# Attention: where the sixteen products of the first values unit stand, and where late weight halves are rounded

## The chip, the cores and the metric

The kernel runs on one core of a Trainium2 chip. The metric is the device time of one execution in microseconds. The kernel before took 3226.36 us in the median of three runs (3222.05 to 3228.58).

## The reference, cut to what matters

Two transformer blocks over 256 tokens of width 2048, in float32. The stage of the change is the sparse attention of the first block:

```python
p = rms_norm(x, g_mix) @ w_in
q = rope(rms_norm(q.reshape(B, S, 8, 128), q_gain), pos)      # 8 heads
k = rope(rms_norm(k.reshape(B, S, 8, 128), k_gain), pos)      # 8 heads
v = v.reshape(B, S, 8, 128)                                   # a plain product, no norm
q_idx = rope(q_idx.reshape(B, S, 16, 64), pos)                # 16 index heads of 64
k_idx = rope(k_idx[:, :, None, :], pos)[:, :, 0]
iscore = einsum('bqhd,bsd->bqhs', q_idx, k_idx)
iscore = einsum('bqhs,bqh->bqs', relu(iscore), w_idx)         # summed over index heads
sel = top_k(iscore, 64)                                       # per query, within its chunk's past
out = softmax(q k[sel] * scale) v[sel]
```

## The kernel before, in words

A product of float32 operands is made on TensorE as three fp32r matmuls: high weight half by high input, high weight half by low input, low weight half by high input. `product(u, k)` issues these three for one 128-row slice k of weight unit u (lines 861 to 863). A unit has 16 slices and gives 128 output features for all 256 tokens in one of four banks `PG`. Below, "a product" is one such triple; "half" is half a unit of weights (128 x 1024). Before a half can be used, ScalarE copies it, rounded (`half_high`, line 647), and VectorE subtracts that copy in place (`half_low`, line 652). Four buffers hold rounded copies, so `half_high(h)` waits until the products of half h-4 are done (`half_done` or `unit_done`, line 646).

The input projection has 60 units. Six of them, units 54 to 59 (`V_UNIT` is 54, `LATE` is 6), are the last values heads; their 96 products are left over for the attention, where `values(lo, hi)` (line 1029) issues products lo to hi-1 of them between other work. Halves 108 to 111 (units 54 and 55) are rounded before the attention; halves 112 to 119 (units 56 to 59) in it.

`attention` on TensorE (line 1034) has these stages, all in program order:

- **Squares**: 16 sums over the head dimension, `ones` by the squares of one q or k head (line 1042, a plain float32 matmul that the trace shows as two records). ScalarE squares head n into one of four buffers (line 1655) and waits for sum n-4; VectorE turns sum n into a mean square (line 2243); TensorE's sum n waits for mean n-2. There are no products here.
- **Rope**: 25 rotations (line 1049), the first 9 for the index queries and keys, the other 16 for q and k. Each is followed by two products. VectorE multiplies the rotated tile by the sine (line 2260) and adds the cosine part of GpSimd (line 2263); TensorE's rotation r waits for tile r-2. For tiles 9 to 24, VectorE first applies the norm (line 2250), which needs ScalarE's Ln and Exp over all mean squares (lines 1658 and 1661, two loads of the activation table). VectorE's queue also has `half_low` of halves 112 to 116 ahead of tiles 5, 9, 13, 17 and 21, and of half 117 behind the last (lines 2253 to 2265). ScalarE's queue has `half_high(112)` behind the four Exp.
- **Index**: after four small transposes (line 1055), 32 index products (line 1066), 64 rows deep: 16 heads with 128 keys for the first 128 queries, then 16 with 256 keys for the rest. Each is followed by one product, and the last 14 of the 96 follow alone (line 1069). ScalarE takes relu (line 1682, four buffers), VectorE adds it weighted (line 2277). After each 16, VectorE finds the 64 largest by eight rounds of max and match-replace (lines 2285, 2286).
- **Heads**: transposes of the values (line 1077), then logits, softmax and values of 16 (head, query tile) pairs, with the first products of the output projection between them (from line 1085). The first softmax step is line 2296 on VectorE, after its top-64 search.

All of it is written out by hand; each engine works through its own queue in order. SyncE loads units in turn into four slots, each when its slot's last unit is done (line 740); ScalarE's queue also issues the load of `x` (line 1689) once all values are taken.

Of the kernel before, what the change touches and what calls it, by code (L numbers as in the profile page):

```python
# [15 lines left out]
KT = D // P  # L16
# [241 lines left out]
LATE = 6  # L258
# [8 lines left out]
V_UNIT = P1_AT[("dsa", DSA_TILES - LATE)]  # L267
# [47 lines left out]
def build(nc, A, out):  # L315
    ctx = ExitStack()
    with ctx:
# [41 lines left out]
        def con(name):  # L359
            return C[:, CON[name][0]:CON[name][1]]  # L360
# [277 lines left out]
        HALVES = 2 * U0["wo"]  # L638
# [127 lines left out]
        def _(pe):  # L766
# [262 lines left out]
            def values(lo, hi):  # L1029

                for m in range(lo, hi):
                    product(V_UNIT + m // KT, m % KT)

            def attention():
# [3 lines left out]
                for n in range(16):  # L1038
                    pe.wait_ge(a_sq, n + 1)
                    if n >= 2:  # L1040
                        pe.wait_ge(a_ms, n - 1)
                    pe.matmul(PX[:, n % 2, 0:T], con("ones"), SQ[:, n % 4, :], start=True, stop=True).then_inc(a_sum, 1)

                for r in range(25):
                    if r >= 9:
                        pe.wait_ge(a_nrm, r - 8)
                    if r >= 2:
                        pe.wait_ge(a_rope, r - 1)
                    pe.matmul(PX[:, 2 + r % 2, 0:T], con("perm64" if r < 9 else "perm128"), DQ[:, r, :],
                              start=True, stop=True).then_inc(a_rot, 1)  # L1050
                    values(2 * r, 2 * r + 2)

                pe.wait_ge(a_rope, 25)
                for tt in range(TT):
                    mm = pe.transpose(PX[:, 2, tt * P:tt * P + P], LO[:, 2, tt * P:tt * P + P], con("ident"))
                    mm = pe.transpose(PX[:, 2, T + 32 * tt:T + 32 * tt + 32], RS[0:32, tt * P:tt * P + P],
                                      con("ident")[0:32, 0:32])
                mm.then_inc(a_vt, 1)
                pe.wait_ge(a_v, 1)

                for n in range(TT * IDX_HEADS):
                    tt, h = n // IDX_HEADS, n % IDX_HEADS
                    rows = slice(64 * (h % 2), 64 * (h % 2) + 64)
                    if n >= 4:
                        pe.wait_ge(a_relu, n - 3)
                    pe.matmul(PX[:, h % 4, 0:(tt + 1) * P], DQ[rows, 1 + h // 2, tt * P:tt * P + P],
                              DQ[rows, 0, 0:(tt + 1) * P], start=True, stop=True).then_inc(a_is, 1)
                    values(50 + n, 51 + n)
                values(82, LATE * KT)

                pe.wait_ge(a_relu, TT * IDX_HEADS)
                wait_taken(pe, V_UNIT + LATE - 1)
# [402 lines left out]
        def _(act):  # L1475
# [169 lines left out]
            def attention():  # L1645
# [6 lines left out]
                for n in range(16):  # L1652
                    if n >= 4:
                        act.wait_ge(a_sum, n - 3)
                    act.activation(SQ[:, n % 4, :], DQ[:, 9 + n, :], ACT.Square).then_inc(a_sq, 1)
                for g in range(4):
                    act.wait_ge(a_ms, 4 * g + 4)
                    ins = act.activation(MSB[:, 4 * g:4 * g + 4, :], MSB[:, 4 * g:4 * g + 4, :], ACT.Ln)
# [7 lines left out]
                    act.activation(DQ[:, DSA_TILES - LATE + q, :], PG[:, u % BANKS, 0:T],  # L1666
                                   ACT.Copy).then_inc(free_bank(u), 1)

                for q in range(3):
                    half_high(act, 2 * (V_UNIT + 2 + q))  # L1670
                    half_high(act, 2 * (V_UNIT + 2 + q) + 1)
                    take_v(q)
# [4 lines left out]
                for n in range(TT * IDX_HEADS):  # L1677
                    keys = (n // IDX_HEADS + 1) * P
                    act.wait_ge(a_is, n + 1)
                    if n >= 4:  # L1680
                        act.wait_ge(a_acc, n - 3)
                    act.activation(RL[:, n % 4, 0:keys], PX[:, n % 4, 0:keys], ACT.Relu).then_inc(a_relu, 1)
                    if n in (8, 16):
                        half_high(act, HALVES - 2 + (n - 8) // 8)
                    if n in (16, 31):
                        take_v(3 + n // 31)
                for q in range(5, LATE):
                    take_v(q)
                act.dma_start(XTOK, A["x"]).then_inc(s_xtok, 16)
                for g in range(4):  # L1690
                    act.wait_ge(a_vt, g + 2)
# [285 lines left out]
        def _(dve):  # L1977
# [259 lines left out]
            def attention():  # L2237
# [12 lines left out]
                    dve.scalar_tensor_tensor(DQ[:, r, :], DQ[:, r, :], vec("q_gain" if n < 8 else "k_gain"),  # L2250
                                             MSB[:, n, :], ALU.mult, ALU.mult).then_inc(a_nrm, 1)

                late = dict(zip((5, 9, 13, 17, 21), range(2 * V_UNIT + 4, HALVES)))
                for r in range(25):
                    if r in late:
                        half_low(dve, late[r])
                    if 9 <= r + 1 < 25:
# [4 lines left out]
                    dve.wait_ge(a_cos, r + 1)  # L2262
                    dve.tensor_tensor(DQ[:, r, :], ROPE_S[:, r % 2, :], ROPE_C[:, r % 4, :], ALU.add) \
                       .then_inc(a_rope, 1)
                half_low(dve, HALVES - 3)
                dve.wait_ge(a_v, 1)
                for tt in range(TT):
                    keys = (tt + 1) * P
                    sc = ISC[:, tt, 0:keys]
                    for h in range(IDX_HEADS):  # L2270
                        n = tt * IDX_HEADS + h
                        dve.wait_ge(a_relu, n + 1)
                        w = WX[:, tt, h:h + 1]
                        if h == 0:
                            dve.tensor_scalar(sc, RL[:, n % 4, 0:keys], w, None, ALU.mult).then_inc(a_acc, 1)
                        else:
                            dve.scalar_tensor_tensor(sc, RL[:, n % 4, 0:keys], w, sc, ALU.mult, ALU.add) \
                               .then_inc(a_acc, 1)
                        dve.wait_ge(a_acc, n + 1)
                        if n in (9, 17):  # L2280
                            half_low(dve, HALVES - 2 + (n - 9) // 8)

                    link(dve.memset(ISC[0:CH, tt, keys - CH:keys], NEG))
                    for n in range(TOP_K // 8):
# [654 lines left out]
```

## Time and profile before

| | |
|---|---|
| median of three runs | 3226.36 us |
| the profiled execution | 3221.9 us, of which the span is 3220.0 us |
| TensorE busy | 3091.0 us (96% of the span), 19592 matmuls |
| VectorE busy | 1972.2 us (61%) |
| ScalarE busy | 1503.4 us (47%) |
| GpSimd busy | 211.7 us (7%) |
| mean granted TensorE clock | 0.972 of 2.4 GHz |
| the attention in the span | 585.3 us (first square) to 752.1 us (next stage's first matmul) |

A busy TensorE is not a fast one: its clock has two levels, 2.4 GHz (shown as 1.00) and 1.2 GHz (0.50), and a matmul at the lower level takes twice as long and is busy all the while. Rows of a timeline give the start, the duration and in brackets the idle time before it with what ended it.

### The profile page before, as it was taken

The page shows a single profiled execution, that of the slowest core. Times are in us where ns is not written, and L with a number is a line of the kernel's source. Part 1 is how long each engine was busy: PE and PEld are TensorE (multiplying, and loading weights), DVE is VectorE, ACT ScalarE, POOL GpSimd, SP SyncE. Part 2 cuts the span into 40 slices and gives each one's busy share as a digit, 9 for nine tenths or more (in the row PEclk, how much of TensorE's full clock was granted, in tenths as well). Part 3 has the DMA queues.
Part 4 walks back from the last instruction along what each step waited for, and adds up shares of the span by engine and source line. Part 5 has one row for each costly group of instructions (what it writes and reads, how often), then busy time and mean ns, then how long its engine had stood idle before and what let it go on. Part 6 is the DMA issues. An engine that isn't in the chain of part 4 may idle for free.

```text
span 3220.0 us, 48239 instructions
## 1 busy us (share of the span) xinstructions
PE 3091.0 (96%) x19592; PEld 2731.4 (85%) x19592; DVE 1972.2 (61%) x2533; ACT 1503.4 (47%) x2079; POOL 211.7 (7%) x263
## 2 busy tenths in 40 slices
PE   8999999899799999999997899999999999999998
PEld 7888898667678887777996789999998989899896
DVE  6555655645577787887558874444665545555454
ACT  5445444424466666665530024764444434344343
POOL 0000000200000000000186600000000000000000
PEclk9999999959999999999998998999999999999999
DMA  5222222213288887887442343445555555555554
GB/s 226 86 99 92 102 95 92 79 66 128 102 319 317 313 324 303 319 308 274 170 175 100 118 147 118 162 169 183 210 193 191 190 185 187 192 184 189 186 189 144
DMA packets 81792, 581.80 MB, mean 181 GB/s; under 512 B 9009, under 2 KB 9265, under 8 KB 12338
## 3 DMA queue, kind: packets, MB, share of 16 engines
q1 hardware_dynamic: 79056, 566.45, 48.6%
q10 hardware_dynamic: 2530, 12.36, 1.0%
q8 instruction: 159, 2.61, 0.3%
q14 instruction: 47, 0.39, 0.1%
HBM read 574.58 MB, written 4.19 MB: 180 GB/s over the span
## 4 chain that ended last, share of the span: by engine, by line
PE 82%; DVE 10%; ACT 3%; POOL 2%; issue 2%; DMA 0%; ACTq 0%; SPq 0%; DVEq 0%; POOLq 0%
PE PG L805 9%; PE PG L803 9%; PE PG L806 8%; PE PG L831 5%; PE PG L830 5%; PE PG L829 5%; PE PG L861 4%; PE PG L1234 4%; PE PG L1235 4%; PE PG L1236 4%; PE PG L863 3%; PE PG L862 3%; PE PX L945 3%; DVE work L2599 2%; DVE ring_r L693 1%
## 5 line engine op out<-in xcount | busy, mean ns | idle before, releaser
L693 DVE TENSOR_TENSOR ring_r<-ring,work_r 128x1024 fp32r<-128x1024 f32 x468 | 553.4, 1225 | 320.3 <-ACT work_r L686 317.0
L686 ACT ACTIVATE work_r<-ring 128x1024 fp32r<-128x1024 f32 x468 | 469.0, 1052 | 481.1 <-PE PG L806 236.1
L693 DVE TENSOR_TENSOR ring_r<-ring,C_r 128x1024 fp32r<-128x1024 f32 x244 | 289.3, 1227 | 222.1 <-ACT C_r L686 218.8
L686 ACT ACTIVATE C_r<-ring 128x1024 fp32r<-128x1024 f32 x244 | 245.0, 1052 | 375.5 <-PE PG L806 255.0
L806 PE MATMUL PG<-work_r,ring_r 128*128 128x256 f32 x1344 | 375.1, 279 | 0.0
L806 PE MATMUL PG<-YT_r,ring_r 128*128 128x256 f32 x1280 | 361.8, 283 | 0.0
L863 PE MATMUL PG<-HT_r,ring_r 128*128 128x256 f32 x960 | 276.5, 288 | 0.0
L806 PEld LDWEIGHTS PG<-work_r,ring_r 128*128 128x128 f32 x1344 | 253.5, 189 | 0.0
L830 PE MATMUL PG<-ring_r,HT_r 128*128 128x512 f32 x624 | 246.7, 395 | 0.0
L806 PEld LDWEIGHTS PG<-YT_r,ring_r 128*128 128x128 f32 x1280 | 244.9, 191 | 0.0
L805 PE MATMUL PG<-work_r,C_r 128*128 128x256 f32 x816 | 227.4, 279 | 0.0
L805 PE MATMUL PG<-work_r 128*128 128x256 f32 x800 | 225.2, 282 | 0.0
L803 PE MATMUL PG<-work_r,C_r 128*128 128x256 f32 x672 | 187.5, 279 | 3.2 <-issue 3.2
L803 PE MATMUL PG<-work_r 128*128 128x256 f32 x672 | 188.9, 281 | 0.0
L863 PEld LDWEIGHTS PG<-HT_r,ring_r 128*128 128x128 f32 x960 | 188.1, 196 | 0.0
L803 PE MATMUL PG<-YT_r,work_r 128*128 128x256 f32 x640 | 181.8, 284 | 4.2 <-DVE HT_r L2631 3.5
L803 PE MATMUL PG<-YT_r,C_r 128*128 128x256 f32 x640 | 183.1, 286 | 0.0
L774 PE MATMUL PG<-HT,ring 128*128 128x256 f32 x768 | 172.7, 388 | 0.0
L774 PEld LDWEIGHTS PG<-HT,ring 128*128 128x128 f32 x768 | 149.0, 195 | 24.4 <-issue 3.9
L861 PE MATMUL PG<-HT_r,YT_r 128*128 128x256 f32 x480 | 155.1, 323 | 11.7 <-DVE XT_r L2004 11.7
L805 PEld LDWEIGHTS PG<-work_r,C_r 128*128 128x128 f32 x816 | 153.3, 188 | 0.1
L805 PEld LDWEIGHTS PG<-work_r 128*128 128x128 f32 x800 | 150.5, 188 | 0.0
(619 smaller groups left out, 7599.4 us busy)
## 6 DMA issues: line engine op xcount, KB each, us to landing
ring<-weights SPq DMA_DIRECT2D x472, 1024.0 KB, 4.8
C<-weights SPq DMA_DIRECT2D x32, 1024.0 KB, 4.9
work<-weights SPq DMA_DIRECT2D x32, 1024.0 KB, 5.1
work<-xT SPq DMA_DIRECT2D x4, 512.0 KB, 7.5
XT<-x ACTq DMA_DIRECT2D x1, 2048.0 KB, 9.7
residual<-XT ACTq DMA_DIRECT2D x4, 512.0 KB, 3.0
XT<-residual ACTq DMA_DIRECT2D x1, 2048.0 KB, 10.8
result<-YT SPq DMA_DIRECT2D x8, 256.0 KB, 4.1
```

The source lines that it names most:

```text
L686: act.activation(w_high(u)[:, c], weights(u)[:, c], ACT.Copy).then_inc(w_hi, 1)
L693: dve.tensor_tensor(w_low(u)[:, c], weights(u)[:, c], w_high(u)[:, c].bitcast(F32), ALU.subtract).then_inc(w_lo, 1)
L774: last = pe.matmul(PG[:, (use + t // 2) % BANKS, (t % 2) * T:(t % 2) * T + T], ring[:, u % RING, (k * tiles + t) * P:(k * tiles + t) * P + P],
L803: pe.matmul(o, wh, high[:, k, :], start=(n == 0 and not (down and t_ % 2)), stop=False, skip_group_check=True)
L805: pe.matmul(o, wh, low[:, k, :], start=False, stop=False, skip_group_check=True)
L806: last = pe.matmul(o, wl, high[:, k, :], start=False, stop=(n == kts - 1), skip_group_check=True)
L829: pe.matmul(o, xh, wh, start=(first and kk == 0), stop=False, skip_group_check=True)
L830: pe.matmul(o, xh, wl, start=False, stop=False, skip_group_check=True)
L831: mm = pe.matmul(o, xl, wh, start=False, stop=(last and kk == 3), skip_group_check=True)
L861: pe.matmul(o, wh, HT_r[:, k, :], start=(k == 0), stop=False, skip_group_check=True)
L863: mm = pe.matmul(o, wl, HT_r[:, k, :], start=False, stop=(k == KT - 1), skip_group_check=True)
L1234: pe.matmul(o, xh, wh, start=(k == 0), stop=False, skip_group_check=True)
```

## The change

The 16 products of unit 54 are put between the squares' sums, one behind each. All later products move up by 16: the rope steps issue products 16 to 65, two more (66, 67) follow the last rotation, four (68 to 71) stand behind the small transposes, and the index products take 72 to 95, one each behind the first 24; the last eight index products have none, and nothing is left for behind them. The halves' rounding moves with it: 112 and 113 on ScalarE behind the squares and ahead of Ln; all others up to 119 in the rope stage; on VectorE ahead of tiles 2, 4, 11, 13, 18, 20, one (118) behind the last tile and one (119) behind index product 5. The values of units 54 to 59 are taken out of their banks at matching places.

```diff
--- before.py
+++ after.py
@@ -1040,6 +1040,7 @@
                     if n >= 2:
                         pe.wait_ge(a_ms, n - 1)
                     pe.matmul(PX[:, n % 2, 0:T], con("ones"), SQ[:, n % 4, :], start=True, stop=True).then_inc(a_sum, 1)
+                    values(n, n + 1)
 
                 for r in range(25):
                     if r >= 9:
@@ -1048,14 +1049,16 @@
                         pe.wait_ge(a_rope, r - 1)
                     pe.matmul(PX[:, 2 + r % 2, 0:T], con("perm64" if r < 9 else "perm128"), DQ[:, r, :],
                               start=True, stop=True).then_inc(a_rot, 1)
-                    values(2 * r, 2 * r + 2)
-
+                    values(16 + 2 * r, 18 + 2 * r)
+
+                values(66, 68)
                 pe.wait_ge(a_rope, 25)
                 for tt in range(TT):
                     mm = pe.transpose(PX[:, 2, tt * P:tt * P + P], LO[:, 2, tt * P:tt * P + P], con("ident"))
                     mm = pe.transpose(PX[:, 2, T + 32 * tt:T + 32 * tt + 32], RS[0:32, tt * P:tt * P + P],
                                       con("ident")[0:32, 0:32])
                 mm.then_inc(a_vt, 1)
+                values(68, 72)
                 pe.wait_ge(a_v, 1)
 
                 for n in range(TT * IDX_HEADS):
@@ -1065,8 +1068,8 @@
                         pe.wait_ge(a_relu, n - 3)
                     pe.matmul(PX[:, h % 4, 0:(tt + 1) * P], DQ[rows, 1 + h // 2, tt * P:tt * P + P],
                               DQ[rows, 0, 0:(tt + 1) * P], start=True, stop=True).then_inc(a_is, 1)
-                    values(50 + n, 51 + n)
-                values(82, LATE * KT)
+                    if 72 + n < LATE * KT:
+                        values(72 + n, 73 + n)
 
                 pe.wait_ge(a_relu, TT * IDX_HEADS)
                 wait_taken(pe, V_UNIT + LATE - 1)
@@ -1653,6 +1656,8 @@
                     if n >= 4:
                         act.wait_ge(a_sum, n - 3)
                     act.activation(SQ[:, n % 4, :], DQ[:, 9 + n, :], ACT.Square).then_inc(a_sq, 1)
+                half_high(act, 2 * V_UNIT + 4)
+                half_high(act, 2 * V_UNIT + 5)
                 for g in range(4):
                     act.wait_ge(a_ms, 4 * g + 4)
                     ins = act.activation(MSB[:, 4 * g:4 * g + 4, :], MSB[:, 4 * g:4 * g + 4, :], ACT.Ln)
@@ -1666,7 +1671,8 @@
                     act.activation(DQ[:, DSA_TILES - LATE + q, :], PG[:, u % BANKS, 0:T],
                                    ACT.Copy).then_inc(free_bank(u), 1)
 
-                for q in range(3):
+                take_v(0)
+                for q in range(1, 4):
                     half_high(act, 2 * (V_UNIT + 2 + q))
                     half_high(act, 2 * (V_UNIT + 2 + q) + 1)
                     take_v(q)
@@ -1680,12 +1686,8 @@
                     if n >= 4:
                         act.wait_ge(a_acc, n - 3)
                     act.activation(RL[:, n % 4, 0:keys], PX[:, n % 4, 0:keys], ACT.Relu).then_inc(a_relu, 1)
-                    if n in (8, 16):
-                        half_high(act, HALVES - 2 + (n - 8) // 8)
-                    if n in (16, 31):
-                        take_v(3 + n // 31)
-                for q in range(5, LATE):
-                    take_v(q)
+                    if n in (12, 31):
+                        take_v(4 + n // 31)
                 act.dma_start(XTOK, A["x"]).then_inc(s_xtok, 16)
                 for g in range(4):
                     act.wait_ge(a_vt, g + 2)
@@ -2250,7 +2252,7 @@
                     dve.scalar_tensor_tensor(DQ[:, r, :], DQ[:, r, :], vec("q_gain" if n < 8 else "k_gain"),
                                              MSB[:, n, :], ALU.mult, ALU.mult).then_inc(a_nrm, 1)
 
-                late = dict(zip((5, 9, 13, 17, 21), range(2 * V_UNIT + 4, HALVES)))
+                late = dict(zip((2, 4, 11, 13, 18, 20), range(2 * V_UNIT + 4, HALVES)))
                 for r in range(25):
                     if r in late:
                         half_low(dve, late[r])
@@ -2262,7 +2264,7 @@
                     dve.wait_ge(a_cos, r + 1)
                     dve.tensor_tensor(DQ[:, r, :], ROPE_S[:, r % 2, :], ROPE_C[:, r % 4, :], ALU.add) \
                        .then_inc(a_rope, 1)
-                half_low(dve, HALVES - 3)
+                half_low(dve, HALVES - 2)
                 dve.wait_ge(a_v, 1)
                 for tt in range(TT):
                     keys = (tt + 1) * P
@@ -2277,8 +2279,8 @@
                             dve.scalar_tensor_tensor(sc, RL[:, n % 4, 0:keys], w, sc, ALU.mult, ALU.add) \
                                .then_inc(a_acc, 1)
                         dve.wait_ge(a_acc, n + 1)
-                        if n in (9, 17):
-                            half_low(dve, HALVES - 2 + (n - 9) // 8)
+                        if n == 5:
+                            half_low(dve, HALVES - 1)
 
                     link(dve.memset(ISC[0:CH, tt, keys - CH:keys], NEG))
                     for n in range(TOP_K // 8):
```

## Rows read from the trace of the kernel before

**Rows 1.** The chain of work that ended last: shares of the span by engine.
```profile
PE 82%; DVE 10%; ACT 3%; POOL 2%; issue 2%; DMA 0%; ACTq 0%; SPq 0%; DVEq 0%; POOLq 0%
```
**Rows 2.** Stretches: PE, PEld, DVE, ACT, POOL busy (count), clock, DMA share, GB/s.
```profile
585.86:592.10 6.24, 6.24 (x14) 3.66 (x15) 3.61 (x7) 3.27 (x9) 3.69 (x4) 0.50 0.08 34
...
609.28:612.60 3.32, 3.32 (x11) 2.96 (x12) 1.95 (x5) 0.72 (x1) 0.70 (x1) 0.50 0.00 0
...
643.40:668.42 25.02, 25.02 (x77) 18.19 (x75) 6.80 (x18) 5.11 (x16) 0.00 (x0) 0.50 0.08 28
668.42:701.68 33.26, 33.26 (x82) 19.50 (x81) 13.94 (x43) 7.62 (x19) 0.00 (x0) 0.50 0.11 42
...
712.80:752.10 39.30, 31.21 (x149) 25.24 (x148) 28.06 (x106) 23.31 (x59) 0.00 (x0) 0.83 0.24 85
```
**Rows 3.** Timeline of TensorE: squares' sums, then rotations.
```profile
585.86 6.93 PE L1042 MATMUL PX<-SQ,C 128*128 128x256 f32 x16 [3.84 <-ACT SQ L1655]
...
597.74 0.59 PE L1049 MATMUL PX<-work,C 128*128 128x256 f32 x2
...
598.88 0.60 PE L1049 MATMUL PX<-work,C 128*128 128x256 f32 x2
...
609.28 1.22 PE L1049 MATMUL PX<-work,C 128*128 128x256 f32 x2 [3.35 <-DVE work L2263]
...
611.58 1.05 PE L1049 MATMUL PX<-work,C 128*128 128x256 f32 x2
```
**Rows 4.** Timelines of ScalarE and VectorE: Ln, Exp, the stall of half 112.
```profile
595.82 1.28 ACT L1658 ACT_TABLE_LOAD   x1
...
602.32 3.90 ACT L1661 ACTIVATE work<-work 128x1024 f32<-128x1024 f32 x4
...
607.20 1.22 DVE L652 TENSOR_TENSOR ring_r<-ring,YT_r 128x1024 fp32r<-128x1024 f32 x1 [3.29 <-ACT YT_r L647]
```
**Rows 5.** Timeline of VectorE: the head of rope tile 9, and the last half.
```profile
613.47 1.22 DVE L652 TENSOR_TENSOR ring_r<-ring,YT_r 128x1024 fp32r<-128x1024 f32 x1
...
641.07 1.22 DVE L652 TENSOR_TENSOR ring_r<-ring,YT_r 128x1024 fp32r<-128x1024 f32 x1
```
**Rows 6.** Timeline of TensorE: small transposes, index products.
```profile
641.21 0.33 PE L1055 MATMUL PX<-C,work 128*128 128x128 f32 x1 [0.48 <-DVE work L2263]
...
642.50 0.49 PE L1066 MATMUL PX<-work 64*128 64x128 f32 x2 [0.35 <-ACT work L1675]
...
643.52 0.79 PE L1066 MATMUL PX<-work 64*128 64x128 f32 x2
...
685.12 1.22 PE L1066 MATMUL PX<-work 64*128 64x256 f32 x2
686.27 0.58 PE L861 MATMUL PG<-HT_r,YT_r 128*128 128x256 f32 x1
```
**Rows 7.** Timeline of VectorE: the two searches, additions, the first softmax step.
```profile
668.40 0.11 DVE L2283 MEMSET work<- 64x64 f32 x1
...
674.45 0.35 DVE L2275 TENSOR_SCALAR work<-work 128x256 f32<-128x256 f32 x1
...
676.49 1.00 DVE L2277 SCALAR_TENSOR_TENSOR work<-work 128x256 f32<-128x256 f32 x2
...
702.02 0.11 DVE L2283 MEMSET work<- 64x64 f32 x1
...
712.80 0.29 DVE L2296 CUSTOM_DVE_ANT_0 work<-PX,work 128x128 f32<-128x128 f32 x1 [2.44 <-PE PX L1085]
```
**Rows 8.** Matmuls of few rows elsewhere: a timeline row, then stretches with clock.
```profile
391.80 0.67 PE L926 MATMUL PX<-work 64*128 64x256 f32 x2 [0.67 <-DVE work L2151]
...
391.80:394.04 2.24, 2.24 (x17) 2.00 (x17) 1.31 (x2) 0.00 (x0) 0.00 (x0) 1.00 0.08 26
...
1961.00:1964.20 3.20, 3.20 (x17) 2.24 (x17) 0.65 (x1) 0.00 (x0) 0.00 (x0) 1.00 0.43 179
1964.30:1967.60 3.30, 3.30 (x11) 2.18 (x10) 0.00 (x0) 0.00 (x0) 0.00 (x0) 0.50 0.00 0
```

## The prediction, made before the result

> **What bounds the kernel now.** I read the page's chain of waits first: TensorE carries 82% of it, so work taken off TensorE or out of its waits counts nearly in full [rows 1]. Then the attention cut into stretches, with the granted clock [rows 2]; then the timelines of three engines at the seams of these stretches. There are three surprises.
>
> First, the index stage (642.5 to 701.7) runs at 1.2 GHz from 643.4 to its end, though TensorE shows busy in all of 25.02 + 33.26 us. The 16 steps with 256 keys take 33.26 us, 2.08 each [rows 2]; the 15 with 128 keys between the starts at 643.52 and 668.42 take 1.66 each [rows 2, 6]. The first step, nearly all at 2.4 GHz, took 1.02 (642.50 to 643.52) [rows 6]. So the clock costs some 0.64 us a step. It fell after a stretch in which TensorE waited twice (0.48 and 0.35 us) around small transposes [rows 6].
>
> Second, in the rope stage VectorE waited 3.29 us for half 112, rounded only behind Exp; TensorE then waited 3.35 us and lost its clock until 612.6 [rows 2 to 4]. From tile 9 on VectorE sets the pace: 613.47 to 641.07 for 16 tiles and four halves [rows 5].
>
> Third, behind the index stage VectorE's second search ends at 712.80 - 2.44 = 710.36, and the first softmax step waits 2.44 us more for the logits, late because 14 products stand ahead of the transposes [rows 7]. So of that tail only 2.44 us can be won; the rest lies beside the search.
>
> **The change, part by part.** All sums use the profiled execution, 3221.9 us (span 3220.0 and 1.9 around it). It is 4.5 us under the median of 3226.4, so I subtract the gain from either and state the median's.
>
> *Squares.* Eight sums took 6.93 us, 0.87 each at 1.2 GHz; a rotation (the same matmul) with two products takes 2.30 at 1.2 GHz (609.28 to 611.58) and 1.14 at 2.4 (597.74 to 598.88) [rows 3]. With one product I take the middle: 1.6 and 0.79. VectorE and ScalarE need about 0.42 a step and lie beside it. The slow clock before lasted 6.24 us from the first sum [rows 2]; I keep that: 3.9 steps, then 12.1 x 0.79 = 9.6, and the stage ends at 592.1 + 9.6 = 601.7 instead of 597.74: +4.0. Bounds: 12.6 us if all is at 2.4 GHz, 25.6 if none is, against 11.9 before.
>
> *Rope, tiles 0 to 8.* Call the end of squares E. ScalarE rounds half 112 beside the last sums, and 113 once product 15 is done, to E + 1.2. From the table load to the end of the first Exp took 595.82 to 603.3, 7.5 us [rows 4], so the first inverse root is there at E + 8.8. TensorE needs 9 x 1.14 = 10.3 for nine steps; VectorE now has two halves (2 x 1.22) among them, worth a slip of 0.8. Rotation 9 starts near E + 11.1, so Ln and Exp stay hidden by about 2 us, and the wait for half 112 with its lost clock is gone. VectorE comes to tile 9 at about E + 11.8 = 613.5. Before: 613.47 [rows 5]. So the 4.0 us that the squares take are given back here, nearly exactly.
>
> *Rope, tiles 9 to 24.* Four halves before, four after, other places: 27.6 us again. ScalarE has each half long before VectorE asks. If one came late, VectorE would wait and everything with it: up to the 1.22 us that a half takes VectorE, for each; I take nothing, since TensorE is then at most four steps from the products that free the buffer. The end stays at 641.1.
>
> *Seam.* Six more products (0.35 each, 2.1 us) fall around the transposes; they fill the two waits of 0.83 us. The index stage starts 1.2 us later, at 643.7, and TensorE no longer waits ahead of it.
>
> *Index.* Two cases, by the clock. If the clock is **kept**: 16 steps of 1.0 end at 659.7. The first search starts there and takes 6.05 us as before (668.40 to 674.45); then 16 additions at 0.50 [rows 7], so VectorE is done not before 674. TensorE's eight steps with product and 256 keys are shown at 1.2 GHz only: between half of 2.08 and 2.08; scaled like the shorter ones (1.02 by 1.66) 1.27, to 669.8. Eight index products alone: 1.15 at 1.2 GHz (685.12 to 686.27) [rows 6], half that at best. With thin work and waits for VectorE's additions I expect the clock lost in the middle of them: about 7 us, to 676.8. The second search starts at 677 instead of 702.02, ends at 685.4, and the transposes (3.5 to 5 us) lie beside it. First softmax step: 685.5 instead of 712.80, -27.3. If the clock is **lost** as before, VectorE's start is 643.7 + 26.6 + 8 x 2.08 + 8 x 1.15 = 696.2, the softmax 704.8: -8.0.
>
> Which? For keeping it: nothing idles at the seam any more; index-like matmuls, 64 rows deep, ran at 2.4 GHz from 391.80 to 394.04, after a wait of 0.67 us [rows 8]. Against: at 1961 to 1964 TensorE never idled, on matmuls of 128 rows and of one row in turn, and the clock fell all the same [rows 8]. Index steps stand between these. I take "kept".
>
> By the Trainium skill (TensorE: Matmul & The Clock Gate, Part 1) the clock goes down after idling and comes back with sustained work; by that rule alone the old index stage would have recovered its clock, since TensorE is shown busy throughout. The trace contradicts it [rows 2]: what fills the engine matters, not only that it is busy.
>
> *Heads.* Before, this stage began at 2.4 GHz and had 0.83 in its mean [rows 2]; now it begins at 1.2 after a search in which TensorE rests. Its first matmuls are short and mostly beside VectorE: +1.3 us, between 0 and 4.
>
> *Loads.* Each unit's slot comes free earlier or as before; the load of `x` starts 30 us earlier and nothing waits for it. Nothing.
>
> Sum, kept: -27.3 + 1.3 = -26 us: 3196 for an execution like the profiled, 3200 at the median.
>
> **Rivals.** *A. The clock is lost at the seam or in the first steps.* The work of a step is unchanged, and it did not hold the clock before. -8.0 + 1.3 = -6.7: 3219. For it: the 1961 stretch; against: the seam's waits are what preceded the fall. *B. Lost midway*, say at the step to 256 keys: 16 fast steps (-10), eight at 2.08; VectorE then starts its search near 686: 3207 to 3212. *C. Slower.* Squares with products do not bring the clock up: fp32 sums and fp32r products alternate with gaps at each turn. All 16 steps at 1.6 give 25.6, +13.7 against before, of which the vanished stall gives back 4; with the clock also lost in the index stage (-6.7) that is +3: 3229. It decides from eleven slow steps more than I count. Against: the same mix at 609.28 to 612.60 was granted 2.4 GHz at its end [rows 2, 3].
>
> **How the numbers follow.** Kept 0.60, B 0.16, A 0.19, C 0.05. The likeliest gives 3200, with 3193 to 3206 as its own range (a step of 1.19 to 1.4, the thin steps 4.5 to 9 us, heads 0 to 4, and the spread of the three runs). Over all cases 3192 to 3221: it leaves out C and some of A. A measurement of this kernel tells 0.2% (6.5 us) from no change. Case A sits on that edge, so half of it is "same"; C at 3229 is inside it too, unless late halves come on top. Faster 0.85, same 0.12, slower 0.03.
>
> **What would show it.** Clock 1.00 in the index stage up to its 24th product, steps of about 1.0 and 1.25; the second search starting near 677; VectorE the one that ends the stage; no wait at half 112; squares ending near 602 and the last rope tile still near 641; one stretch at 1.2 GHz fewer at 609. I am wrong if the clock in the index stage is 0.50 although nothing idled ahead of it (then 3219), or if the rope stage ends after 643, which would mean that Ln and Exp came late behind half 113.

## The result, and the profile after

The kernel after took 3190.30 us in the median (3187.62 to 3194.78, 16 executions). The kernel before took 3218.57 us in the same comparison (3192.52 to 3228.58, 16 executions). The ratio is 0.9938, 95% interval [0.9912, 0.9963]: faster by 0.4 to 0.9%.

That interval is wide for a reason that the first three times of the kernel before did not show. Its sixteen executions form two groups with nothing between them: seven at 3192.5 to 3196.9 us and nine at 3218.3 to 3228.6. The three on which the prediction rested (3222 to 3229) all belong to the upper one, and so does the profiled one. The kernel after has one group. So there are two gains to tell apart: some 32 us against the upper group (its median is 3222.6), and some 3 us against the lower (3193.5). The difference of 28.3 us between the two medians is neither: the median of the kernel before (3218.57) is the mean of its eighth and ninth time, the two lowest of the upper group, and one execution more in the lower group would have put it into the gap.

The profiled execution after took 3189.36 us, its span 3187.5 us. The page's engine totals hardly moved (TensorE is 34 us less busy with the same matmuls):

```profile
span 3187.5 us, 48239 instructions
PE 3057.0 (96%) x19592; PEld 2712.3 (85%) x19592; DVE 1973.8 (62%) x2533; ACT 1503.1 (47%) x2079; POOL 213.8 (7%) x263
...
PE 82%; DVE 11%; ACT 3%; POOL 2%; issue 2%; DMA 0%; ACTq 0%; SPq 0%; DVEq 0%; POOLq 0%
```

The same stretches as in [rows 2], with the same columns: squares at the lower clock, the other squares, rope, the index steps with 128 keys, those with 256, and the heads:

```profile
586.30:589.40 3.10, 3.05 (x10) 2.72 (x11) 1.86 (x3) 1.57 (x5) 3.04 (x4) 0.50 0.17 71
589.50:600.46 10.96, 10.96 (x71) 10.24 (x71) 5.68 (x14) 5.12 (x11) 0.55 (x1) 1.00 0.01 1
600.46:640.30 39.84, 33.59 (x208) 28.94 (x206) 38.36 (x74) 18.64 (x21) 17.02 (x21) 1.00 0.24 82
642.83:658.20 15.37, 15.37 (x81) 11.38 (x80) 6.38 (x17) 4.73 (x17) 0.00 (x0) 1.00 0.19 69
658.24:670.30 12.06, 12.03 (x57) 7.48 (x56) 10.89 (x38) 4.97 (x14) 0.00 (x0) 1.00 0.12 26
681.43:719.00 37.57, 29.37 (x149) 23.84 (x149) 28.09 (x106) 23.42 (x59) 0.00 (x0) 0.86 0.13 42
```

The number behind the five busy times, the granted clock, is 1.00 in both index stretches, where it was 0.50. In rope VectorE is busy 38.36 of 39.84 us: it sets the pace there.

TensorE's timeline: squares, the one wait among the first nine rotations, the seam, two index steps of each size, the bare eight, the transposes, the second pair of heads, and the next stage's first matmul:

```profile
586.35 1.19 PE L1042 MATMUL PX<-SQ,C 128*128 128x256 f32 x2 [3.84 <-ACT SQ L1658]
...
587.99 1.05 PE L1042 MATMUL PX<-SQ,C 128*128 128x256 f32 x2
...
589.44 0.60 PE L1042 MATMUL PX<-SQ,C 128*128 128x256 f32 x2
...
608.38 0.70 PE L1050 MATMUL PX<-work,C 128*128 128x256 f32 x2 [0.60 <-DVE work L2265]
...
640.40 0.27 PE L1057 MATMUL PX<-C,work 128*128 128x128 f32 x1
...
642.83 0.48 PE L1069 MATMUL PX<-work 64*128 64x128 f32 x2
643.25 0.39 PE L861 MATMUL PG<-HT_r,YT_r 128*128 128x256 f32 x1
...
658.24 0.70 PE L1069 MATMUL PX<-work 64*128 64x256 f32 x2
658.87 0.39 PE L861 MATMUL PG<-HT_r,work_r 128*128 128x256 f32 x1
...
659.42 0.70 PE L1069 MATMUL PX<-work 64*128 64x256 f32 x2
...
667.64 2.69 PE L1069 MATMUL PX<-work 64*128 64x256 f32 x16
671.80 1.07 PE L1080 MATMUL PX<-C,work 128*128 128x128 f32 x8 [1.48 <-ACT work L1671]
...
681.98 0.79 PE L1088 MATMUL PX<-work 128*128 128x128 f32 x2 [6.04 <-DVE work L2300]
...
718.90 0.66 PE L829 MATMUL PG<-work_r,HT_r 128*128 128x512 f32 x1 [2.47 <-DVE ring_r L693]
```

Against [rows 6]: the bracket is gone at the small transposes (640.40) and at the first index product (642.83).

VectorE's timeline, the rows that answer to [rows 4, 5, 7]: halves 112 and 113 without a bracket, then the two searches and the first softmax step:

```profile
603.06 1.21 DVE L652 TENSOR_TENSOR ring_r<-ring,YT_r 128x1024 fp32r<-128x1024 f32 x1
...
606.24 1.21 DVE L652 TENSOR_TENSOR ring_r<-ring,YT_r 128x1024 fp32r<-128x1024 f32 x1
...
658.61 0.11 DVE L2285 MEMSET work<- 64x64 f32 x1
...
668.86 4.13 DVE L2279 SCALAR_TENSOR_TENSOR work<-work 128x256 f32<-128x256 f32 x8 [0.19 <-ACT work L1688]
673.06 0.11 DVE L2285 MEMSET work<- 64x64 f32 x1
...
681.43 0.29 DVE L2298 CUSTOM_DVE_ANT_0 work<-PX,work 128x128 f32<-128x128 f32 x1
```

The eight additions in one group with 0.19 us of waiting say that VectorE, not TensorE, ends this stage, and the softmax step has no bracket: it follows the search at once. From the first square's sum to the first softmax step is 681.43 - 586.35 = 95.08 us, before it was 126.94 [rows 3, 7]: -31.9. From there to the next stage's first matmul is 37.5 us, before 39.3 [rows 2]: -1.8. The whole span is 32.5 us shorter, so the rest of the kernel took about 1 us more.

### The profile page after: what moved, and what is told of

It is laid out like the page before. It is cut to its first block, busy times and chain, and to the rows that moved or that the text cites. A ratio compares the mean times of both kernels' runs of the same rounds, so it can differ in the third digit from the quotient of the medians.

```text
span 3187.5 us, 48239 instructions
## 1 busy us (share of the span) xinstructions
PE 3057.0 (96%) x19592; PEld 2712.3 (85%) x19592; DVE 1973.8 (62%) x2533; ACT 1503.1 (47%) x2079; POOL 213.8 (7%) x263
## 4 chain that ended last, share of the span: by engine, by line
PE 82%; DVE 11%; ACT 3%; POOL 2%; issue 2%; DMA 0%; ACTq 0%; SPq 0%; DVEq 0%; POOLq 0%
PE PG L805 9%; PE PG L803 9%; PE PG L806 9%; PE PG L830 6%; PE PG L831 5%; PE PG L829 5%; PE PG L1237 4%; PE PG L1238 4%; PE PG L1239 4%; PE PG L861 4%; PE PG L863 3%; PE PG L862 3%; PE PX L945 3%; DVE work L2601 2%; DVE ring_r L693 1%
```

## The experiments

Each has twelve executions, but for before_look, which is a single one. The kernels of one part below ran on one chip, beside executions of the kernel before; only in the last part pairs ran on another chip than the other two. As the kernel before has two groups, a ratio against it mixes both; where a few us matter I compare medians and groups, and between chips a difference of 1 to 2 us says little (the kernel after had medians of 3190.3 and 3188.8 on two). The kernel before was in its lower group in 13 of 29, 20 of 35 and 17 of 34 executions (one outlier left out), beside the 7 of 16 above: half of all. By default an edit is shown against the kernel after.

### Is it the clock at the seam?

**before_look**: the kernel before, unchanged, one profile.

> The kernel before, unchanged. Its 16 executions fall into two groups, 3192.5 to 3196.9 us (7) and 3218.3 to 3228.6 (9); the profiled one lay in the second and lost the clock at the first index product. Theory S (the seam decides: two short waits of TensorE around the small transposes tip the clock or not, from execution to execution): an execution near 3194 has clock 1.00 through the index stage, with steps of 0.96 and 1.18 us, one near 3222 has 0.50 there. Rival R (the fast group comes from another stage): the index stage is at 0.50 in both.

It took 3193.6 us: an execution of the lower group. Its index stage, in the columns of [rows 2]:

```profile
642.25:657.70 15.45, 15.45 (x81) 11.40 (x81) 6.46 (x17) 5.29 (x17) 0.00 (x0) 1.00 0.12 38
657.70:676.50 18.80, 18.80 (x83) 11.50 (x83) 14.01 (x44) 7.39 (x19) 0.00 (x0) 1.00 0.18 61
```

and its seam on TensorE:

```profile
640.96 0.33 PE L1055 MATMUL PX<-C,work 128*128 128x128 f32 x1 [0.48 <-DVE work L2263]
...
642.25 0.49 PE L1066 MATMUL PX<-work 64*128 64x128 f32 x2 [0.35 <-ACT work L1675]
...
723.55 0.60 PE L829 MATMUL PG<-work_r,HT_r 128*128 128x512 f32 x1 [2.48 <-DVE ring_r L693]
```

The last row is the next stage's first matmul. VectorE's first softmax step:

```profile
686.10 0.29 DVE L2296 CUSTOM_DVE_ANT_0 work<-PX,work 128x128 f32<-128x128 f32 x1 [0.72 <-PE PX L1085]
```

The same program, the same two waits of 0.48 and 0.35 us, the same matmuls, and the clock is 1.00 instead of 0.50. From the first index product to the first softmax step it took 686.10 - 642.25 = 43.9 us against 712.80 - 642.50 = 70.3 [rows 6, 7]. These 26.4 us are most of the 29 between the medians of the two groups. Another 1.9 lie in the heads: 723.55 - 686.10 = 37.45 us here against 39.3 [rows 2].

In the profile of [rows 2], from the upper group, the clock did not come back among the index steps. It came back once products stood in a row: the last index product starts at 699.72, and in the tail of products behind it the matmuls shorten again:

```profile
704.45 0.42 PE L862 MATMUL PG<-XT_r,work_r 128*128 128x256 f32 x1
704.67 0.33 PE L863 MATMUL PG<-HT_r,ring_r 128*128 128x256 f32 x1
704.83 0.28 PE L861 MATMUL PG<-HT_r,work_r 128*128 128x256 f32 x1
```

**seam_only**: the kernel before with nothing changed but six products put at the seam.

```diff
+                values(50, 52)              # behind the last rotation
...
+                values(52, 56)              # behind the small transposes
...
-                    values(50 + n, 51 + n)
-                values(82, LATE * KT)
+                    values(56 + n, 57 + n)
+                values(88, LATE * KT)
```

> The kernel before with nothing changed but the seam: products 50 and 51 behind the last rotation, 52 to 55 behind the small transposes, the index products take 56 to 87, eight follow alone. Theory S: the index stage keeps 2.4 GHz in every execution, so all times lie within 5 us of the fast group of before: 3191 to 3198, no second group, and about 1 us under that group's. Rival M (the clock is kept because the squares' products and the mended half-112 stall change what ran before, not because of the seam): times stay in two groups as before, median 3215 to 3222.

Median 3192.72 us (3190.70 to 3195.11, 12 executions), one group; ratio 0.9951 [0.9923, 0.998].

**no_seam**: the kernel after without those six.

```diff
-                values(66, 68)
...
-                values(68, 72)
...
-                    if 72 + n < LATE * KT:
-                        values(72 + n, 73 + n)
+                    if 66 + n < LATE * KT:
+                        values(66 + n, 67 + n)
...
-                    if n in (12, 31):
+                    if n in (14, 31):
```

> The changed kernel without its six products at the seam: the index products take 66 to 95 instead, so TensorE waits around the small transposes as before. Theory S: two groups of executions again, one near 3190 (kept), one near 3212 (lost: steps of 1.66 and 2.08, 30 of them with products). Rival M: one group near 3190, clock kept in all.

Two groups again: six executions at 3190.2 to 3193.1 and six at 3211.8 to 3219.6; median 3202.43, ratio 0.9991 [0.9954, 1.0028]. The profiled one belongs to the upper, and its index stage shows what [rows 2] did:

```profile
643.70:665.80 22.10, 22.10 (x68) 16.27 (x68) 5.84 (x15) 4.15 (x15) 0.00 (x0) 0.50 0.07 25
```

So the six products at the seam put all twelve executions into the lower group, with or without the rest of the change; the other parts of the change (squares, halves, a shorter tail) don't do it. That each of these executions kept its clock is read from the times, the profiles show one of each kernel.

### Which of the six?

**seam_two**: only the two ahead of the transposes. **seam_four**: only four, behind them.

```diff
                 values(66, 68)              # seam_two keeps it
...
-                values(68, 72)              # seam_two drops it
-                    if 72 + n < LATE * KT:
-                        values(72 + n, 73 + n)
+                    if 68 + n < LATE * KT:
+                        values(68 + n, 69 + n)
```

```diff
-                values(66, 68)
...
-                values(68, 72)
+                values(66, 70)              # seam_four, behind the transposes
...
+                    if 70 + n < LATE * KT:
+                        values(70 + n, 71 + n)
```

> The changed kernel with only the two products behind the last rotation kept at the seam (66, 67); the index products take 68 to 95. TensorE's first wait (0.48 us) is filled, the second (0.35) is not. Theory S1 (the work around the whole seam counts, thin matmuls and waits together, so two products already tip it): one group near 3190. Theory S2 (any wait next to the small transposes can tip the clock): two groups, near 3190 and 3214.

> The changed kernel with only the four products behind the small transposes kept (66 to 69); the index products take 70 to 95. The first wait stays, the second is filled. S1: one group near 3190. S2: two groups.

seam_two has two groups, 3187.3 to 3190.5 (6) and 3210.6 to 3215.6 (6), median 3200.56, ratio 0.9986 [0.9949, 1.0022]. Its profiled execution, one of the upper group, lost the clock at 643.9, 2.5 us behind the one wait that was left:

```profile
640.14 0.28 PE L1057 MATMUL PX<-C,work 128*128 128x128 f32 x1
...
641.38 0.49 PE L1068 MATMUL PX<-work 64*128 64x128 f32 x2 [0.35 <-ACT work L1680]
...
643.72 0.49 PE L861 MATMUL PG<-HT_r,YT_r 128*128 128x256 f32 x1
644.01 0.42 PE L862 MATMUL PG<-XT_r,YT_r 128*128 128x256 f32 x1
...
644.57 0.79 PE L1068 MATMUL PX<-work 64*128 64x128 f32 x2
```

The first of the three matmuls at 643.72 is still partly fast, the next takes 0.42 where it took 0.28, the next index product 0.79 instead of 0.49. seam_four has one group, 3188.0 to 3194.0, median 3191.44, ratio 0.994 [0.991, 0.997], though the longer wait stays:

```profile
640.21 0.33 PE L1056 MATMUL PX<-C,work 128*128 128x128 f32 x1 [0.48 <-DVE work L2264]
...
642.71 0.48 PE L1068 MATMUL PX<-work 64*128 64x128 f32 x2
```

The four products between the small transposes and the first index product decide; the two ahead of the transposes show no effect on it (six of twelve in the upper group, as without any). Whether the four act by filling the wait of 0.35 us or by standing dense (1.5 us of back-to-back products) between two thin pieces of work was not told apart.

### Does the work of the index steps matter?

**dense**: no_seam with two products behind each of the first 15 index products and none behind the other 17, so the seam keeps both waits.

```diff
-                    if 66 + n < LATE * KT:
-                        values(66 + n, 67 + n)
+                    if 66 + 2 * n < LATE * KT:
+                        values(66 + 2 * n, 68 + 2 * n)
```

> The kernel without the filled seam, with two products behind each of the first 15 index products and none behind the other 17. Theory D (with more products a step the clock comes back once lost): executions that lose it at the seam have it again within some 7 us, so all lie within 6 us of each other, near 3190 to 3196. Rival: two groups as without it, near 3191 and 3215.

One group, median 3192.15 us (3189.75 to 3196.73), ratio 0.9963 [0.9933, 0.9992]. The profiled execution never fell in the index steps:

```profile
642.10:661.90 19.80, 19.77 (x120) 16.00 (x120) 6.36 (x16) 4.44 (x16) 0.00 (x0) 1.00 0.19 73
```

So with the waits in place, denser steps keep all executions in one group, as a filled seam does. The median is 3.4 us above that of the kernel after on the same chip (3188.75, below). Whether some executions fall and come back within a few steps, or none falls, one profile doesn't say (it is the fastest of the twelve); the times fit both.

**thin**: the kernel after with a product behind every second index product only, and eight behind the last.

```diff
-                    if 72 + n < LATE * KT:
-                        values(72 + n, 73 + n)
+                    if n % 2 == 0:
+                        values(72 + n // 2, 73 + n // 2)
+                values(88, LATE * KT)
...
-                    if n in (12, 31):
+                    if n in (16, 31):
```

> The changed kernel, seam filled, but the index products have one product behind every second one (16) and eight follow behind the last. Theory W (what fills TensorE in the index stage holds the clock): the clock falls inside the stage although TensorE never idles; two index products at 1.2 GHz with one product take about 2.4 us (128 keys) and 3.2 (256 keys), so the stage needs some 45 us less what it keeps: 3198 to 3206. Rival I (only idling takes the clock): kept, the first search starts 4 us sooner: 3184 to 3187.

The theory that thin steps lose the clock by themselves was not borne out: median 3185.69 us (3183.11 to 3189.39), ratio 0.9938 [0.9906, 0.997], 3.1 us under the kernel after on the same chip. The clock held through all of the first stretch, and fell only once TensorE had waited 3.02 us for a relu buffer:

```profile
642.44:654.90 12.46, 12.46 (x84) 8.61 (x83) 9.63 (x31) 5.49 (x21) 0.00 (x0) 1.00 0.25 85
658.61:668.00 9.39, 9.39 (x28) 5.37 (x28) 6.31 (x13) 3.51 (x10) 0.00 (x0) 0.50 0.00 1
```

Here too it came back only when products stood in a row, at 670.9, in the tail of products behind the last index product (666.98). The steps were also less thin than I meant, because two index products in a row take hardly longer than one (next part).

### What are the other parts worth?

**after_again**: the kernel after, unchanged, beside the next kernel. **late_halves**: halves 112 and 113 rounded behind the four Exp, as the kernel before had it for 112.

```diff
-                half_high(act, 2 * V_UNIT + 4)    # ahead of Ln
-                half_high(act, 2 * V_UNIT + 5)
...
+                half_high(act, 2 * V_UNIT + 4)    # behind Exp
+                half_high(act, 2 * V_UNIT + 5)
```

> The changed kernel, unchanged, beside the others of this call: 3188 to 3195, one group, as in its first 16 executions.

> The changed kernel with halves 112 and 113 rounded behind the four Exp again; VectorE still asks for 112 ahead of rope tile 2. Theory H (the rounding's place on ScalarE is worth the stall): VectorE waits about 5.5 to 6.5 us ahead of tile 2, TensorE about as long, and the clock is lost for one slice; the inverse roots come earlier but nothing waits for them: 3196 to 3198, index stage still at 2.4 GHz in all. Rival: the wait is taken up by slack in the rope stage, which VectorE paces only from tile 9 on: 3190 to 3192.

The kernel after took 3188.75 us again (3185.45 to 3194.62), one group, ratio 0.9969 [0.9943, 0.9994]. late_halves took 3196.01 (3191.40 to 3202.16), ratio 0.9972 [0.994, 1.0004]: 7.3 us more. The profiled execution is its slowest (3202.16). The next two fences show VectorE and then TensorE in it:

```profile
608.93 1.23 DVE L652 TENSOR_TENSOR ring_r<-ring,YT_r 128x1024 fp32r<-128x1024 f32 x1 [5.83 <-ACT YT_r L647]
```

```profile
611.01 1.22 PE L1050 MATMUL PX<-work,C 128*128 128x256 f32 x2 [5.84 <-DVE work L2265]
```

VectorE stood 5.83 us, TensorE with it, and the rotations after that ran at 1.2 GHz (granted 0.50 from 611 to 617). So with VectorE's halves in their new places, ahead of tiles 2 and 4, the early rounding is worth 7.3 us; without it the kernel is 3.8 us above the lower group of the kernel before on the same chip (3192.3). Early rounding without products in the squares, and late rounding with VectorE's halves in their old places, were not run.

### Is there a better order?

In the kernel after an index product of 64 rows alone takes 0.42 us to the next matmul (642.83 to 643.25 above), and the bare eight with 256 keys took 2.69 us, 0.34 each, where one ahead of a product takes 0.63 (658.24 to 658.87). Neighbouring heads use opposite halves of the array's rows (lines 1066 to 1071 of the kernel after: rows 0 to 63 for even heads, 64 to 127 for odd ones). So **pairs**: two index products, then two products.

```diff
-                    if 72 + n < LATE * KT:
-                        values(72 + n, 73 + n)
+                    if n % 2 and 72 + n < LATE * KT:
+                        values(71 + n, 73 + n)
```

> The changed kernel with the index products in pairs (heads of rows 0 to 63 and 64 to 127 back to back) and then two products. In the changed kernel's trace eight bare index products of 256 keys took 2.69 us, 0.34 each, while a single one takes 0.63 to the next product. Theory P (two matmuls on different row halves overlap, and the gap at each turn between kinds is paid once per pair): the 16 steps with 128 keys fall from 15.4 to about 10 us, the first search starts 5 us sooner, VectorE sets the rest: 3185. Rival Q (the bare ones were fast only since nothing followed; no overlap): 3189 to 3190.

Median 3184.11 us (3180.68 to 3187.90), ratio 0.9933 [0.9904, 0.9962]: 6.2 us under the first median of the kernel after, which is from another chip, and 9.1 us under the lower group of the kernel before on its own (3193.3). TensorE's timeline:

```profile
642.91 0.49 PE L1069 MATMUL PX<-work 64*128 64x128 f32 x4
643.34 0.39 PE L861 MATMUL PG<-HT_r,YT_r 128*128 128x256 f32 x1
...
644.23 0.49 PE L1069 MATMUL PX<-work 64*128 64x128 f32 x4
...
655.07 0.70 PE L1069 MATMUL PX<-work 64*128 64x256 f32 x4
655.70 0.38 PE L861 MATMUL PG<-HT_r,work_r 128*128 128x256 f32 x1
```

Two index products now take 0.43 us (642.91 to 643.34), as long as one did, and two with 256 keys 0.63 (655.07 to 655.70), again as one did. With its two products a pair costs 1.32 us (642.91 to 644.23) instead of 1.92. The Trainium skill (TensorE: Matmul & The Clock Gate, Part 3) says this: matmuls that use different row groups of the array run at the same time. The trace agrees.

The gain is spent early, though, as VectorE's two searches show:

```profile
653.91 0.11 DVE L2285 MEMSET work<- 64x64 f32 x1
...
668.20 0.11 DVE L2285 MEMSET work<- 64x64 f32 x1
```

The first starts at 653.91 instead of 658.61 (-4.7), but the second at 668.20 instead of 673.06 (-4.9), no sooner for it, since VectorE needs 0.52 for each of its 256-key additions. To see whether pairs among the 256-key steps bring anything, **pairs_first** has them in the first sixteen only; **pairs_again** repeats pairs beside it.

```diff
-                    if 72 + n < LATE * KT:
+                    if n < IDX_HEADS:
+                        if n % 2:
+                            values(71 + n, 73 + n)
+                    elif 72 + n < LATE * KT:
                         values(72 + n, 73 + n)
```

> The changed kernel with index products in pairs for the first 128 queries only, single ones after. In the kernel with pairs throughout, TensorE was done early with the 256-key pairs, waited 1.11 us for the first search and lost the clock at 662.5, 14 us before the heads. If that costs (theory), this keeps the clock to about 670 and the heads start warmer: 3182 to 3184, 1 to 2 us under the pairs. Rival: VectorE sets the end of both, nothing gained: the same as pairs, 3184.

> The kernel with pairs throughout, unchanged, beside the one with pairs for the first queries only: 3181 to 3188, median 3184.

pairs_first: 3184.67 us with one outlier of 3370.59 in it, 3184.37 without (3180.85 to 3187.12), ratio 0.9926 [0.9894, 0.9957]. pairs_again: 3184.90 (3178.97 to 3186.73), ratio 0.9929 [0.9899, 0.9958]. The same: behind the first search VectorE sets the end, and a faster TensorE finds nothing to win. Even the clock shows no effect on the time there. In the profiled execution of pairs it fell among the bare eight (mean granted clock 0.66 from 660.85 to 665.80), which took 4.86 us; in that of pairs_first it held (1.00 from 660 to 668) and they took 2.69 as in the kernel after. The medians are the same within 0.8 us. The row of pairs:

```profile
660.85 4.86 PE L1069 MATMUL PX<-work 64*128 64x256 f32 x16 [1.11 <-ACT work L1688]
```

Either is the best version found, 4 to 6 us under the kernel after and 7 to 9 under the lower group of the kernel before. thin, which has pairs of index products too, lies within 1.6 us of them, on another chip.

## Why the prediction was right, and where it was not

The sign was right and the mechanism was the one forecast as likeliest; the size was not quite. The forecast was 3200 us, with a range of 3192 to 3221. The median is 3190.3, 9.7 us under the forecast and 1.7 us under the range. That the difference of the two medians (28.3 us) comes near the forecast gain of 26 is luck in part: the forecast priced an execution of the kernel before that loses the clock, and nine of the sixteen did. Against such executions the gain is 32 us, against the others 3. By the prediction's own steps, in the profiled execution:

| step | predicted | measured |
|---|---|---|
| squares end | 601.7 | 600.5 |
| rotation 9 starts | 11.1 later | 11.5 later (611.9) |
| first inverse root | 8.8 later | 8.8 later (609.3) |
| last rope tile, VectorE | 641.1 | 640.2 |
| index stage starts | 643.7 | 642.8 |
| step with 128, 256 keys | 1.0, 1.27 | 0.96, 1.18 |
| first search | 660 | 658.6 |
| bare eight index products | 7 us | 2.7 us |
| second search | 677 | 673.1 |
| first softmax step | 685.5 | 681.4 |
| heads | +1.3 | -1.8 |

*Squares.* The cost of a sum with a product was right (predicted 1.6 and 0.79, measured 1.64 for the first and 0.79 at the higher clock, fourteen steps from 589.44 to 600.46). What was off is how long the lower clock lasts: I kept the 6.24 us of before, it was 3.1, and the squares with products came up after two steps. That this is not fixed shows in the profile of pairs, which has the same squares and took four slow steps. Two slow steps fewer are worth some 1.6 us (an estimate from these two costs), and the range's bound of 12.6 to 25.6 us was hit near its low end (14.1). Against the 11.9 us of before the stage costs 2.2 us more, not 4.0. Rival C, that this mixture never comes up, is refuted.

*Rope.* The forecast holds within 0.4 us a step. The stall of half 112 is gone; the first nine rotations slip by 1.2 us, 0.60 of it one wait, where 0.8 was forecast. From the end of the squares to the last half the stage takes 39.7 us, before 43.3 [rows 3, 5]: 3.6 us given back, more than the squares cost. late_halves shows that this isn't free by itself: with the halves left behind Exp it costs 7.3 us.

*Seam and clock.* "Nothing idles at the seam any more" was the argument for keeping the clock, and seam_only, no_seam, seam_two and seam_four bear it out in part: the six products do it, four of them suffice, and the longer of the two waits does no harm once the four stand behind it. Where the prediction was wrong is in taking a lost clock for a property of the kernel before. It is a coin: half of the executions of one program lose it. Rival A was argued from "the work of a step did not hold the clock before"; in before_look the same work held it.

*Index tail: the mis-sized term.* I scaled an index product alone from 1.15 us at 1.2 GHz and expected the clock lost among the bare eight: 7 us. They took 2.69 at the higher clock, 4.3 less. By an estimate from the prediction's own figures about half of that is the clock, the other half that the eight overlap in twos: even the prediction's "half that at best", eight times 0.57 = 4.6 us, was too much. VectorE's additions, forecast as a bound of "not before 674", now end the stage, at 673.1, so only 2.7 of the 4.3 us reach the softmax step.

*Heads.* The stage did begin at 1.2 GHz after the second search, and still took less: TensorE is busy 31.2 of 39.3 us there before [rows 2] and 29.4 of 37.6 after. The term was wrong by 3.1 us, because it was added to the 39.3 us of a profile in which the stage was itself long. In before_look, without the change and with a mean clock of 0.91 there, the stage took 37.45 us, as long as after (37.47): the change and the lower clock at its start cost it nothing that shows. Of the fourteen profiles ten have 37.4 to 37.7 us for this stage and four 39.2 to 39.3 (before, no_seam, seam_two and seam_four, the last of which had kept its clock in the index stage). What makes it long in those four is open.

The sum of the misses in the profiled executions, from the first sum on: 1.9 us up to the first search (squares 1.7 of it), 2.7 in the tail, 3.1 in the heads, less 1.2 that the rest of the kernel took more: 6.5, which is the step from the forecast 3195.9 for the profiled execution to its 3189.4. The remaining 3 us are the start value: 3226.4 is 3.8 us above the median of its own group.

What the change is worth, put together from the runs: the seam's products turn all executions into ones that keep the clock, 26 to 29 us in half of them, less than 1 us in the rest (seam_only at 3192.7 against 3193.3 for the lower group beside it). Everything else (squares, halves, a shorter tail) is worth the distance from seam_only to the kernel after, 2.4 to 4 us (3192.7 against 3190.3 and 3188.8, on different chips). Behind these few us stand two index stages at the same clock: from the first index product to the second search the kernel before took 34.8 us in before_look (642.25 to 677.04), the kernel after 30.2 (642.83 to 673.06), while the time from the first sum to the first index product is the same in [rows 3, 6] and after (56.6 and 56.5), with 22 products more in it.

**Still open.** Why the clock is lost in one execution and kept in the next, with the same waits and the same work; which property of the four products holds it; whether dense recovers from a loss or never has one; and what makes the heads 1.8 us longer in four of the profiles.

## What to carry to other kernels

Take more than three times of a kernel before you argue from one profile: a profiled stretch at 1.2 GHz in a busy engine may be in only half of the executions, and then a change there is worth half of what the profile says. Ahead of a stage of thin matmuls, put a microsecond or two of dense ones that have to be done anyway behind the small pieces at its entry, and see in many executions whether the slower group is gone; here it was, in one kernel and at one seam. And size a run of half-height matmuls from rows where they stand alone in a row, not from one between products.

## What the runs showed of the hardware

- TensorE is shown busy without a gap and stays at 1.2 GHz for 58.28 us [rows 2], in some executions; in others of the same program it stays at 2.4 GHz over the same matmuls. What tips it is small: 1.5 us of dense products ahead of the stage, or denser steps in it. Where it did come back at this place, TensorE had products in a row and nothing else (at 704.8 in the kernel before, at 670.9 in thin). The Trainium skill (TensorE: Matmul & The Clock Gate, Part 1) has the clock fall behind long idle gaps and come back under sustained work; here it fell behind two waits of 0.48 and 0.35 us (before), or the second alone (seam_two), and did not come back while index products stood between the others, with TensorE busy throughout.
- Two plain float32 matmuls of 64 rows on opposite halves of the array take as long as one: 0.43 us for two with 128 keys where one took 0.42, and 0.63 for two with 256 keys where one took 0.63 (pairs and the kernel after); eight in a row with 256 keys take 0.34 each.
- The clock after a wait: it was down behind one of 3.02 us (thin) and one of 5.84 us (late_halves); it stayed up over one of 0.60 us in the rope stage of the kernel after, and over 0.48 and 0.35 us in before_look.
